# Chunked recurrence on one core: the 64x64 products of the triangular inverse placed on all four quarters of the array, the identity moved into stationary operands, two products in place of three Horner steps

## The reference

```python
def step(S, inp):
    r_t, w_t, k_t, v_t, kk_t, a_t = inp
    sa = jnp.einsum('bhvk,bhk->bhv', S, -kk_t)
    S = S * w_t[:, :, None, :] + sa[..., None] * (kk_t * a_t)[:, :, None, :] + v_t[..., None] * k_t[:, :, None, :]
    return S, jnp.einsum('bhvk,bhk->bhv', S, r_t)
```

## Time and profile before

| | |
|---|---|
| median of three runs | 1868.63 us (1867.83 to 1869.66) |
| profiled execution, first to last instruction | 1865.4 us; its own time is not listed beside it |
| PE busy, share of the span | 1830.1 us, 98% |
| DVE, ACT, POOL busy | 950.1, 793.7, 412.2 us |
| granted TensorE clock, mean | 0.998 of full |

### The profile page before, as it was taken

The page is one execution under the profiler, slowest core; times in us unless marked ns, Lnnn a source line. Parts: engine busy times, 40 slices in busy tenths (PEclk is TensorE's granted clock), DMA queues, the critical chain, the costliest instruction groups (busy, mean ns, idle before and its releaser), DMA issues.

```text
span 1865.4 us, 37306 instructions
## 1 busy us (share of the span) xinstructions
PE 1830.1 (98%) x15533; PEld 1483.5 (80%) x15533; DVE 950.1 (51%) x2056; ACT 793.7 (43%) x1725; POOL 412.2 (22%) x415
## 2 busy tenths in 40 slices
PE   9999999999999999999999999999999999999998
PEld 8997766888887789877877878778787886667887
DVE  5677766233444354135555565555653357775523
ACT  5346666343444433224343343433432346655421
POOL 5650000111112431222222222222221301101221
PEclk9999999999999999999999999999999999999999
DMA  5153310234323333330221221212213220005442
GB/s 192 47 172 90 86 40 1 97 96 140 106 88 111 114 124 94 114 110 32 82 63 60 69 64 59 72 56 77 64 43 98 88 81 19 1 1 181 149 156 90
DMA packets 146000, 159.81 MB, mean 86 GB/s; under 512 B 15093, under 2 KB 123961, under 8 KB 145833
## 3 DMA queue, kind: packets, MB, share of 16 engines
q1 hardware_dynamic: 145800, 157.37, 26.4%
q0 software_dynamic: 32, 0.07, 0.0%
HBM read 110.53 MB, written 52.62 MB: 87 GB/s over the span
## 4 chain that ended last, share of the span: by engine, by line
PE 93%; ACT 3%; DVE 2%; POOL 1%; issue 1%; DMA 0%; DVEq 0%; POOLq 0%; ACTq 0%
PE ps L998 9%; PE ps L696 7%; PE ps L1000 7%; PE ps L999 7%; PE ps L697 7%; PE ps L698 7%; PE ps L1109 4%; PE ps L811 3%; PE ps L790 3%; PE ps L890 3%; PE ps L1146 3%; PE ps L892 3%; PE ps L891 3%; PE ps L798 3%; PE ps L1295 3%; PE ps L1318 2%
## 5 line engine op out<-in xcount | busy, mean ns | idle before, releaser
L2820 POOL TENSOR_TENSOR t<-t,t 128x512 fp32r<-128x512 f32 x183 | 238.4, 1316 | 848.0 <-ACT t L1422 828.2
L998 PE MATMUL ps<-t,t 128*128 128x512 f32 (+2 forms) x720 | 291.0, 404 | 1.5 <-POOL t L2820 1.5
L696 PE MATMUL ps<-t,t 128*128 128x256 f32 (+2 forms) x872 | 282.3, 324 | 1.7 <-ACT t L1429 1.0
L697 PE MATMUL ps<-t,t 128*128 128x256 f32 (+2 forms) x872 | 276.5, 317 | 0.0
L698 PE MATMUL ps<-t,t 128*128 128x256 f32 (+2 forms) x872 | 276.4, 317 | 0.0
L1000 PE MATMUL ps<-t,t 128*128 128x512 f32 (+2 forms) x720 | 268.3, 373 | 0.0
L999 PE MATMUL ps<-t,t 128*128 128x512 f32 (+2 forms) x720 | 267.7, 372 | 0.0
L696 PEld LDWEIGHTS ps<-t,t 128*128 128x128 f32 x872 | 165.7, 190 | 18.3 <-issue 6.9
L698 PEld LDWEIGHTS ps<-t,t 128*128 128x128 f32 x872 | 165.7, 190 | 10.4
L697 PEld LDWEIGHTS ps<-t,t 128*128 128x128 f32 x872 | 165.9, 190 | 10.2 <-issue 0.4
L998 PEld LDWEIGHTS ps<-t,t 128*128 128x128 f32 x720 | 135.8, 189 | 30.0 <-issue 7.7
(11 more groups left out here) (278 smaller groups left out, 3285.5 us busy)
## 6 DMA issues: line engine op xcount, KB each, us to landing
t<-in_w_in SPq DMA_DIRECT2D x53, 512.0 KB, 5.9
zgate_spill<-t SPq DMA_DIRECT2D x20, 512.0 KB, 3.0
tile_bias<-t SPq DMA_DIRECT2D x16, 576.0 KB
t<-tile_bias SPq DMA_DIRECT2D x8, 1152.0 KB, 5.8
t<-zgate_spill SPq DMA_DIRECT2D x16, 512.0 KB, 4.1
feat_spill<-t SPq DMA_DIRECT2D x13, 512.0 KB, 3.2
tile_bias<-band_bias SPq DMA_DIRECT2D x48, 128.0 KB
t<-values_and_gates SPq DMA_DIRECT2D x96, 64.0 KB
```

The lines of the kernel that those rows point to most:

```text
L696: e.matmul(dst, lh, rh, start=k == 0, stop=False)
L697: e.matmul(dst, lh, rl, start=False, stop=False)
L998: e.matmul(dst, lh, rh, start=k == 0, stop=False)
L2820: e.tensor_tensor(WLO[wslot(b)][:, o], WST[:, o], WHI[wslot(b)][:, o].bitcast(F), ALU.subtract).then_inc(w_lo.sem, w_lo.up((b, p)))
```

## The change

- From `n4` on, the eight 64x64 products go through `crossed`. It writes two banks: the two chunks of each pair with x = 0 go to the lower bank with row half and column half alike, those with x = 1 to the upper bank with row half and column half exchanged, so that four consecutive products use four different quarters. The data of x = 1 so change their partition half with each product; `turned` says whether the product reads or writes the exchanged side.
- `z` and what follows it are `crossed` too, eight 64x64x128 products each. BD and BF, 128 wide and zeroed by POOL, go; BD, IF, FT and FN of 64 columns take their place.
- Sums with the identity are put into stationary operands: (I + N2), (I + N4), (I + N8) and (I + F) are made by POOL (`e2`, `e4`, `if`, beside `d1`) or by DVE on its way out of PSUM (`e8`, `i2`), and PSUM then holds the finished factor, which is only copied.
- The three Horner steps become (I + F^2)(I + F)Z: product `fn` (F transposed), product `f2`, `z1` and `z2`. One `INV_US` step less: a unit has 26 steps.
- `turned_gram` computes the four matrices NOT for x = 1 on the exchanged side.
- Copies out of PSUM: ACT takes `n2`, `n2t`, `n4t`, `n4`, `d2`, then the transposed F, `z` and `fn` behind one wait for `z`; DVE takes `e8`, `d3`, `x`, `d4`, `i2`, `z1`, `z2`.

```diff
+                def turned_gram(ps):
+                    for m in range(MP):
+                        for q in range(2):
+                            to = 64 * (1 - q)
+                            i = e.matmul(ps[1][to:to + 64, 384 + 64 * m:448 + 64 * m], AR[64:128, 0, 2 * m + q, :], BK[64:128, 2 * m + q, 0, :], start=True, stop=True)
+                def crossed(key, ps, first, turned, lhs, rhs, width=64):
+                    for m in range(MP):
+                        for x, q in ((0, 0), (0, 1), (1, 0), (1, 1)):
+                            of = 64 * (q ^ (x & turned))
+                            to = 64 * (q ^ (x & (1 - turned)))
+                            pq = slice(of, of + 64)
+                            i = e.matmul(ps[x][to:to + 64, first + width * m:first + width * m + width], lhs[pq, MP * x + m], rhs(pq, MP * x + m), start=True, stop=True)
+                    i.then_inc(inv_mm.sem, inv_mm.up((u, key)))
...
-                blocks("n4", mine("n4", (inv_a, (u, "n4"))), whole(B4), whole(B3))
-                blocks("n4t", mine("n4t", (inv_v, (u, "n4t"))), whole(B3), whole(B4))
-                blocks("d2", mine("d2", (inv_v, (u, "d2"))), whole(B4), whole(B5))
+                ps = mine_two("four", (inv_a, (u, "d2")))
+                crossed("n4", ps, 0, 0, B4, whole(B3))
+                crossed("n4t", ps, 128, 0, B3, whole(B4))
+                crossed("d2", ps, 256, 0, S.IF, whole(B5))
...
-                full("z", S.BD, ZA_)
-                for it in range(3):
-                    full(f"z{it}", S.BF, ZB_ if it == 0 else ZA_)
+                ps = mine_two("first", (inv_a, (u, "fn")))
+                crossed("f", ps, 0, 1, NOT, whole(S.BD))
+                crossed("fn", ps, 128, 1, S.BD, whole(NOT))
+                crossed("z", ps, 256, 1, S.BD, whole(ZA_), 128)
+                yield INV_US
+                ps = mine_two("second", (inv_v, (u, "z1")))
+                w.wait_ge(*inv_a[u, "fn"])
+                crossed("f2", ps, 0, 0, S.FN, whole(S.FT))
+                w.wait_ge(*prep_p[u, "if"])
+                crossed("z1", ps, 256, 0, S.IF, whole(ZB_), 128)
+                yield INV_US
+                ps = mine_two("third", (inv_v, (u, "z2")))
+                w.wait_ge(*inv_v[u, "z1"])
+                crossed("z2", ps, 0, 1, B4, whole(ZA_), 128)
...
+                w.wait_ge(*inv_mm[u, "z"])
+                crossed_out("ft", "first", 0, S.FT[:, :, :])
+                crossed_out("z", "first", 256, ZB_[:, :, :], 128)
+                crossed_out("fn", "first", 128, S.FN[:, :, :])
...
+                w.wait_ge(*inv_a[u, "ft"])
+                plus_one(S.IF, S.FT, "if")
```

More of the change, by code:

```diff
@@ L1128, in unit @@
+                crossed("d2", ps, 256, 0, S.IF, whole(B5))
                 yield GRAM_US
+                ps = mine_two("eight", (inv_v, (u, "x")))
                 w.wait_ge(*gram_v[u, "rkt"])
                 w.wait_ge(*prep_a[u, "turn", "v"])
-                blocks("x", mine("x", (inv_a, (u, "x"))), whole(AKT), lambda pq, x: VNN[pq, x % MP, 64 * (x // MP):64 * (x // MP) + 64])
+                crossed("x", ps, 0, 0, AKT, lambda pq, x: VNN[pq, x % MP, 64 * (x // MP):64 * (x // MP) + 64])
                 w.wait_ge(*inv_a[u, "n4"])
-                w.wait_ge(*inv_v[u, "n4t"])
@@ L1134, in unit @@
-                blocks("n8t", mine("n8t", (inv_a, (u, "n8t"))), whole(ND), whole(NDT))
-                w.wait_ge(*inv_v[u, "d2"])
-                blocks("d3", mine("d3", (inv_v, (u, "d3"))), whole(NDT), whole(B6))
+                crossed("n8t", ps, 128, 1, ND, whole(NDT))
+                w.wait_ge(*inv_a[u, "d2"])
+                w.wait_ge(*prep_p[u, "e4"])
+                crossed("d3", ps, 256, 1, S.FT, whole(B6))
                 yield GRAM_US
-                w.wait_ge(*inv_a[u, "n8t"])
+                ps = mine_two("d4", (inv_v, (u, "d4")))
@@ L1139, in unit @@
                 w.wait_ge(*inv_v[u, "d3"])
-                blocks("d4", mine("d4", (inv_v, (u, "d4", 1))), whole(B3), whole(B5))
+                crossed("d4", ps, 0, 0, S.FN, whole(B5))
                 yield INV_US
[L1143 to L1147, removed]
+                ps = mine_two("first", (inv_a, (u, "fn")))
@@ L1759, in unit, with alone @@
                 yield GRAM_US
-                yield GRAM_US
[L1762 to L1769, removed]
+                def alone(key, first, dst):
+                    pv = psum((u, "n2 both"))[:, first:first + 64 * CU_].rearrange("p (x c) -> p x c", x=CU_)
+                    e.activation(dst[:, :, :], pv, ACT.Copy).then_inc(inv_a.sem, inv_a.up((u, key)))
@@ new lines, in crossed_out @@
+                def crossed_out(key, two, first, dst, width=64):
+                    pv = psum_two(lambda x: (u, (two, x)), first, MP * width).rearrange("p x (m c) -> p x m c", c=width)
+                    e.activation(dst.rearrange("p (x m) c -> p x m c", x=2), pv, ACT.Copy).then_inc(inv_a.sem, inv_a.up((u, key)))
+                w.wait_ge(*prep_p[u, "d1"])
+                w.wait_ge(*inv_mm[u, "n2t"])
+                alone("n2", 0, B3)
+                alone("n2t", 256, B4)
+                yield GRAM_US
@@ L1770, in unit @@
+                w.wait_ge(*inv_mm[u, "d2"])
+                crossed_out("n4t", "four", 128, NDT[:, :, :])
+                crossed_out("n4", "four", 0, ND[:, :, :])
+                crossed_out("d2", "four", 256, B6[:, :, :])
                 yield GRAM_US
-                w.wait_ge(*inv_mm[u, "n4t"])
-                blocks_out("n8t", B3)
-                blocks_out("x", ZA_[:, :, 64:128])
                 yield GRAM_US
                 yield INV_US
-                w.wait_ge(*inv_mm[u, "f"])
@@ L2500, in unit, with crossed, by_head, plus_one @@
                 yield GRAM_US
[L2502 to L2508, removed]
+                one = bc(mask(C_I64, MP), 1, 2)
+                def crossed(two, first, width=64):
+                    return psum_two(lambda x: (u, (two, x)), first, MP * width).rearrange("p x (m c) -> p x m c", c=width)
+                def by_head(dst):
+                    return dst.rearrange("p (x m) c -> p x m c", x=2)
+                def plus_one(key, two, first, dst):
+                    e.tensor_tensor(by_head(dst[:, :, :]), crossed(two, first), one, ALU.add).then_inc(inv_v.sem, inv_v.up((u, key)))
+                def copied(key, two, first, dst, width=64):
+                    e.tensor_copy(by_head(dst), crossed(two, first, width)).then_inc(inv_v.sem, inv_v.up((u, key)))
                 gram(1, 0, AKT, C_MS, "akt")
@@ L3322, in unit @@
                     yield GRAM_US
-                for _ in range(5):
+                for _ in range(4):
                     yield INV_US
```

117 lines of the change are left out of this document (55 added, 62 removed).

## The result

| | before | changed |
|---|---|---|
| median | 1868.25 us (1867.83 to 1869.66, 4 runs) | 1836.23 us (1835.57 to 1837.72, 4 runs) |
| profiled span | 1865.4 us | 1834.5 us |

The ratio is 0.9829, with a 95% interval of 0.9815 to 0.9843: 32.0 us less. In another series the same changed kernel gave 1837.63 us, ratio 0.9836 (0.9823 to 0.9848). One run of all, of the kernel with the slots 16 apart, took 2177.99 us at a granted clock of 0.752 and counts in no ratio.

What follows compares the result with a forecast made beforehand. PE, busy 98% of the span, was taken as the bound. 46.7 us saved, less 5.3 for dense restarts and 12.5 of new waits, plus 3.1 of old waits gone, made 32.0 off 1868.6: 1836.6 us, range 1820 to 1851.

Steps and rivals of the forecast that it cites:

- PE work removed and added: Inverse of each unit: 7.80 us of PE work go, 4.88 come; 2.92 saved a unit, 46.7 us for 16.
- The shared bank: Rival, 5%: in `crossed`, quarters writing one bank don't overlap; 10.9 us more PE work than before, 1887 us.
- The dearer dense triples: Two dense triples take 1.58 us after quarter products, 1.47 after full-array groups; three steps a unit change, 5.3 us in all.
- New waits: PE's waits on handovers of the inverse: 12.5 us new, bounds 0 and 25; old waits of 3.1 us go.
- slot 1: `first` to `second`: ACT copies `ft`, `z`, `fn` behind the other slot's step 1; PE waits 0.8 us eight times, 6.4 us.
- scattered delays of ACT: Dense evictions and weight splits now and then stand ahead of a copy on ACT: 0.15 us a unit, 2.4 us.
- Slot 0: `first` to `second`: a single dense triple doesn't cover the three ACT copies in five of eight units, 0.5 us each, 2.5 us.
- between `four` and `eight`: Same two banks, so `x` waits for all three ACT copies; four rounds have a single triple: about 1.2 us.
- The table load: On ACT, no drain accompanies a load of 1.28 us; by the skill's rule the time would be some 22 us longer.
- the cover holds: Rival, 17%: dense triples still cover the copies, no new wait at all; 1817 to 1825 us.
- The copies did not become the bound: Rival, 10%: ACT and DVE come 0.35 us later at each of seven handovers a unit, 39 us; 1855 to 1875 us.
- The step that is gone: A unit declares 0.6 us less; about 14 dense triples move from the rounds to `rest`, at no cost or gain.

Runs made afterwards that it cites:

- the kernel of 27 steps: The changed kernel with an empty fifth inversion step after the last product, so a unit has 27 steps as before: 1835.80 us, ratio 0.9825.
- more cover: The changed kernel with each inversion step declared as 1.0 us instead of 0.6, about 38 more dense triples between the inverse's products: 1827.07 us, ratio 0.9780.
- the Horner steps: The changed kernel with three Horner steps on four quarters in place of the two products, a unit again having 27 steps: 1839.37 us, ratio 0.9843.

## Why the prediction held

**PE work removed and added.** The first step, that PE is the bound and its work counts, stands: two quarters instead of four cost 49.5 us. The added groups were put at 4.88 us a unit. They are 0.86 for each group of 48 (said: 0.89), 0.39 for `d4` (0.38), 1.06 for the first (1.07), 0.84 for the second (0.82), 0.60 for `z2` (0.56) and 0.23 for the turned grams (0.27): 4.84. The lower bound of the 128-column price was not reached. The units end 38 us earlier (the last spread product starts at 1411.01 in place of 1449.44), where the prediction had some 40, and PE is busy 571.1 us in them, where it had 550 to 580.

**The shared bank.** By the Trainium skill (TensorEngine Tiling (Array Packing), Gotcha 1: PSUM Pressure) different row tiles can't access a bank at the same time. Here they do, at the same 0.86 us with shared and with separate banks. In both kernels they write different partitions; what happens on the same ones no run here shows.

**The dearer dense triples** (5.3 us) were put somewhat too high, and their mechanism was told the wrong way round. I had put the cost behind a group on quarters. The changed kernel's timeline has two triples of 1100.50 - 1099.01 = 1.49 us right behind a group on quarters, with a full-array product after them, and 1097.95 - 1096.36 = 1.59 us ahead of one. It is the entry into the quarters that costs 0.10 us, nearly whatever stood before: over both traces the two triples take 1.59 us from quarters to quarters, 1.57 from full-array products to quarters, 1.50 from quarters to full-array products and 1.47 between full-array products (the commonest values). `z1` with `f2` and `z2` have such an entry anew: 2 x 0.10 x 16 = 3.2 us. Three more groups on quarters with 0.02 us behind each add 1, so about 4 us stand in place of 5.3. By the sum PE busy should have fallen by 46.7 - 5.3 = 41.4 us; it fell by 43.1, and by 41.1 in the other series, so the busy time can't tell the two sizes apart.

**New waits.** Said: 12.5 us new, 3.1 old ones gone, 9.4 more idle time. Measured: 12.2 more. For slot 1 the working was close in time: from L1055's start at 1095.33 PE stood before `f2` 5.67 us later (1101.69 - 0.69 - 1095.33; said 5.6) and could go on after 6.36 (said 6.4). It came to 7.0 us in six units instead of 6.4 in eight. What I had as scattered delays of ACT (2.4 us) is part of these 7.0: the dense evictions ahead of three of the waits, some 1.8 us. So the meeting with step 1 by itself cost less than the 6.4 that it was given. Slot 0 was put at 2.5 us and is 1.5, four waits of 0.37 instead of five of 0.5. The 1.2 us between `four` and `eight` are at most 0.8, three waits of 0.16 and two gaps of 0.14. In all the inverse waits 9.5 us (8.9 for ACT, 0.6 for DVE), 3.0 less than the 12.5. On the other side the preparation, the norms and the chain wait longer, for the bonus product 5.4 instead of 3.3, the spread 3.4 instead of 1.8, the chain 2.0 instead of 1.1: 4.6 us that the sum lacks. These errors partly cancel. So do 1.7 us more of PE work gone than said, and the 1.1 us by which the medians fell more than the spans. That the time came out within 0.4 us is luck; the steps deserve a few us.

**Its cause.** I had named exp ahead of the copies, due to the shift by one step. That the shift is to blame is refuted by the kernel of 27 steps: it puts step 0 in the place of step 1, and the copies wait as long. That ACT's work for the other slot stands between the first group and its copies is shown from two sides, by the exp one step later and by the slots 16 apart.

**The table load.** The trace of the changed kernel again has no drain with it: load at 1096.13, 1.28 us, activation at 1097.43; and ahead of the second load the activation ends at 1098.57, with the load at 1098.59. That is against the Trainium skill (ScalarE: Activation LUTs, What ACT_TABLE_LOAD costs), by which 1.38 us more would pass.

**The rivals.** That the cover holds is refuted by 8.9 us of waits on the copies. The copies did not become the bound: PE is still busy 97% of the span. The step that is gone cost and gave nothing on balance (27 steps: 1835.80).

The lowest median of the study is that of the change with exp one step later, 1825.73 us; more cover, 1827.07, can't be told from it.

## What to carry to other kernels

Where TensorE is full, 64x64 products on two quarters are worth placing on all four, even if every intermediate has to change its partition half each time: here that was worth 49.5 us, while the new algebra, the identities and the copies without the quarters made the kernel slower. A shorter group on TensorE has less behind it to cover the copies, so look on the copying engine's program at what stands just ahead of them, and move that first. Declaring more cover between the steps takes the same wait away as moving the work does, and both together (with half the extra cover) gained nothing more. An experiment that changes the order of two programs needs a partner with the same order: beside the kernel of 27 steps the Horner steps look otherwise than beside the change.

## What was not expected of the hardware

Two dense triples take 1.57 to 1.59 us when products on quarters follow and 1.47 to 1.50 when a full-array product does; what stood before them makes only 0.02 or 0.03 of it. It is a cost of 0.10 us that a timeline shows in the group ahead of the one that causes it. Four quarters run twice as fast as two even at 64 columns: 16 and 48 instructions take 0.39 and 0.86 us, 15 ns for each further one, against 29 ns on two quarters.
